# Delta gates computed in pieces inside the delta layer's input projection, and another order of ScalarE's steps in attention

## What is computed

```python
def deltanet_mixer(h, s0_fwd, s0_bwd, w_in, conv_w, a_log, dt_bias, norm_g, w_o):
    proj = h @ w_in                       # 4096 columns of q, k, v, z and 32 columns of gates
    qkv, z, gate_a, gate_b = jnp.split(proj, [...], axis=-1)
    ...
    log_decay = -jnp.exp(a_log) * jax.nn.softplus(gate_a + dt_bias)
    beta = jax.nn.sigmoid(gate_b.astype(jnp.float32).reshape(b, t, 2, DN_HEADS))
    o_f, s_f = gated_delta_chunked(q, k, v, log_decay[:, :, 0], beta[:, :, 0], s0_fwd)
    ...

def gated_delta_chunked(q, k, v, g, beta, s0):   # chunks of 64 tokens
    g = jnp.cumsum(g, axis=-1)            # within a chunk; exp(g), exp(g_last - g), exp(g_last) follow
    ...

def one_block(q_blk):                     # attention, 128 queries at a time
    s = jnp.einsum('bqhgd,bkhd->bhgqk', q_blk, k).astype(jnp.float32) * scale
    p = jax.nn.softmax(s, axis=-1).astype(v.dtype)
    return jnp.einsum('bhgqk,bkhd->bqhgd', p, v)
```

## Time and profile before

| | us |
|---|---|
| median of three runs | 5915.29 |
| lowest and highest run | 5910.57, 5921.78 |
| the profiled execution's own time | 5911.5 |
| its span, first to last instruction | 5909.7 |
| TensorE busy in the span | 5230.6 (89%) |
| VectorE, ScalarE, GpSimd busy | 2408.0, 1886.3, 593.0 |
| mean granted TensorE clock | 0.931 |

### The profile page before, as it was taken

The page is one execution under the profiler, slowest core; times in us unless marked ns, Lnnn a source line. Parts: engine busy times, 40 slices in busy tenths (PEclk is TensorE's granted clock), DMA queues, the critical chain, the costliest instruction groups (busy, mean ns, idle before and its releaser), DMA issues. The chain is left out here.

```text
span 5909.7 us, 148888 instructions
## 1 busy us (share of the span) xinstructions
PE 5230.6 (89%) x66464; PEld 4736.3 (80%) x66464; DVE 2408.0 (41%) x4332; ACT 1886.3 (32%) x3895; POOL 593.0 (10%) x1104
## 2 busy tenths in 40 slices
PE   6797999988998887999885887899887999988998
PEld 2386888877997766999884776799877888877997
DVE  0242454534334364333214553433452545544334
ACT  1032343333223354222323332322322443433223
POOL 0002232200000000000002221000001232310000
PEclk8798999988998898999896997899998999988999
DMA  9731000011221301221322111122021000011221
GB/s 406 316 116 45 23 19 22 17 54 58 79 71 50 65 2 58 79 72 50 111 77 64 39 44 69 51 74 75 32 108 63 21 17 25 15 43 56 79 71 53
DMA packets 99690, 411.65 MB, mean 70 GB/s; under 512 B 18011, under 2 KB 33755, under 8 KB 69918
## 3 DMA queue, kind: packets, MB, share of 16 engines
q1 hardware_dynamic: 87590, 376.71, 18.4%
q10 hardware_dynamic: 11520, 26.22, 1.1%
HBM read 358.20 MB, written 39.44 MB: 67 GB/s over the span
## 5 line engine op out<-in xcount | busy, mean ns | idle before, releaser
L372 PE MATMUL bank<-src_hi,ring_hi 128*128 128x320 f32 x4032 | 933.2, 313 | 177.0 <-DVE ring_lo L353 128.5
L372 PE MATMUL bank<-src_lo,ring_hi 128*128 128x320 f32 x4032 | 929.8, 312 | 4.7 <-issue 4.7
L372 PE MATMUL bank<-src_hi,ring_lo 128*128 128x320 f32 x4032 | 928.0, 312 | 0.0
L372 PEld LDWEIGHTS bank<-src_hi,ring_hi 128*128 128x128 f32 x4032 | 683.3, 191 | 184.7 <-issue 171.8
L372 PEld LDWEIGHTS bank<-src_hi,ring_lo 128*128 128x128 f32 x4032 | 683.9, 190 | 5.0 <-issue 5.0
L372 PEld LDWEIGHTS bank<-src_lo,ring_hi 128*128 128x128 f32 x4032 | 684.5, 191 | 0.0
L592 ACT ACTIVATE stage<-bank 128x320 f32<-128x320 f32 x512 | 196.2, 435 | 1398.4 <-PE bank L372 1398.4
L364 DVE TENSOR_TENSOR ring_lo<-ring,ring_hi 128x2048 fp32r<-128x2048 f32 x178 | 407.5, 2289 | 521.4 <-ACT ring_hi L360 520.5
L372 PE MATMUL bank<-hidden_hi,ring_lo 128*128 128x320 f32 x2048 | 466.7, 309 | 0.0
L372 PE MATMUL bank<-hidden_hi,ring_hi 128*128 128x320 f32 x2048 | 466.5, 309 | 0.0
L372 PE MATMUL bank<-hidden_lo,ring_hi 128*128 128x320 f32 x2048 | 466.5, 309 | 0.0
(11 more groups left out here) (396 smaller groups left out, 8607.8 us busy)
## 6 DMA issues: line engine op xcount, KB each, us to landing
ring<-w_mlp SPq DMA_DIRECT2D x124, 1024.0 KB, 4.8
mod_ring<-w_mod SPq DMA_DIRECT2D x48, 2048.0 KB, 11.8
ring<-rw_wrkv SPq DMA_DIRECT2D x22, 1024.0 KB, 5.1
rkv<-stage ACTq DMA_DIRECT2D x48, 320.0 KB, 2.6
ring<-dn_win SPq DMA_DIRECT2D x15, 1024.0 KB, 5.3
r_k<-rkv SPq DMA_DIRECT2D x32, 320.0 KB, 3.4
dn_proj<-stage ACTq DMA_DIRECT2D x32, 320.0 KB, 3.9
src<-mixed SPq DMA_DIRECT2D x24, 320.0 KB, 7.3
```

Of the source, the lines that this page charges most:

```text
L372: last = self.nc.tensor.matmul(acc[h][:, 0:HALF], wt[:, n % 2, k, m * P:(m + 1) * P], x[:, k, h * HALF:(h + 1) * HALF], start=first and q ...
```

## The change

Two edits. In attention, ScalarE's order within a step becomes: copy of (n, 0), both exponentials of n + 1, copy of (n, 1).

```diff
                     for n in range(NPT):
-                        for e in range(2):
-                            if n + 1 < NPT:
+                        transposed_out(n, 0)
+                        if n + 1 < NPT:
+                            for e in range(2):
                                 exponentials(n + 1, e)
-                            transposed_out(n, e)
+                        transposed_out(n, 1)
```

```diff
-                    projection(nc, g, d["dn_win"], 16, out=d["dn_proj"])
-                    delta_gates(nc, g)
+                    delta_input(nc, g, d["dn_win"], d["dn_proj"])
...
+def delta_input(nc, g, w, out):
+    N_SLABS, DEEP = 16, 2
+    RATES, TIMES, SUMS_AT, ENDS, NEGATED, TURNED = 4, 5, 7, 9, 10, (11, 12, 13, 14)
...
+        tmp = ed[:, :].rearrange("p (a t) -> p a t", a=2)
...
+        acc, raw_l, raw_c, turned = [(bank[0], bank[1]), (bank[2], bank[3])], bank[4], bank[5], bank[6:8]
...
+                for n in range(1, N_SLABS):                      # SP
+                    ring.load(sp, 0, 0, n)
+                    if n == 4:
+                        sp.wait_ge(s["raw_out"], 1)
+                        sp.dma_start(g.d["dn_gates"]..., raw[0:4 * DN_HEADS, :]).then_inc(s["raw_stored"], 16)
+                        sp.wait_ge(s["raw_stored"], 16)
+                        for a in range(2):
+                            sp.dma_start(ab[H8, a, :, :], ...).then_inc(s["raw_loaded"], 16)
...
+                for n in range(N_SLABS):                         # TensorE
+                    if n:
+                        pe.wait_ge(s["wl_ready"], n + 3)
+                    for m in range(2):
+                        u = 2 * n + m
+                        pe.wait_ge(s["evacuated"], u + 1)
+                        for k in range(NB):
...
+                            last = ring.product(acc[u % DEEP], n, m, k, x_hi, x_lo, k == 0, k == NB - 1)
+                        last.then_inc(s["mm_done"], 1)
+                    if n == 1:
+                        gate_sums()
+                    if n in TURNED:
+                        turn_rows(TURNED.index(n))
...
+                def evacuate(u):                                 # ScalarE
+                    act.wait_ge(s["mm_done"], u + 5)
+                    if u >= DEEP:
+                        act.wait_ge(s["stored"][u % DEEP], 16 * (u // DEEP))
+                    for h in range(2):
+                        last = nc.scalar.copy(stage[:, u % DEEP, h * HALF:(h + 1) * HALF], acc[u % DEEP][h][:, 0:HALF])
+                    last.then_inc(s["evacuated"], 1)
+                    act.wait_ge(s["evacuated"], u + 1 + DEEP)
+                    act.dma_start(out[u], stage[:, u % DEEP, :]).then_inc(s["stored"][u % DEEP], 16)
...
+                for n in range(N_SLABS):
+                    if n + 1 < N_SLABS:
+                        ring.upper(act, 0, 0, n + 1)
+                    evacuate(2 * n)
+                    if n == 2:
+                        raw_gates()
+                    if n == TIMES:
+                        rates()
+                    if n == ENDS:
+                        decays()
+                    evacuate(2 * n + 1)
+                    if n == TIMES:
+                        betas()
+                    if n in TURNED:
+                        columns_out(TURNED.index(n))
...
+                for n in range(N_SLABS):                         # VectorE
+                    if n + 1 < N_SLABS:
+                        ring.rest(dve, 0, 0, n + 1)
+                    if n == RATES:
+                        rate_inputs()
+                    if n == SUMS_AT:
+                        running_sums()
+                    if n == NEGATED:
+                        dve.wait_ge(s["decays"], 2)
+                        nc.vector.tensor_scalar(nb[H8, :], rows[H8, R_EG:R_EG + TT], -1.0, ...).then_inc(s["scaled"], 3)
```

More of the change, by code:

```diff
@@ L2273, in _ @@
             def _(sp):
[L2274 to L2280, removed]
+                ring.load_first(sp, FRONT)
@@ L2287, in _ @@
+                sp.wait_ge(s["gates_stored"], 16 * (DN_HEADS + 1))
             @block.tensor
             def _(pe):
[L2289 to L2293, removed]
@@ L2320, in _, with raw_gates @@
[L2320 to L2325 removed]
+                def raw_gates():
+                    act.wait_ge(s["raw_ps"], 1)
+                    nc.scalar.copy(raw[0:4 * DN_HEADS, S_LAT], raw_l[0:4 * DN_HEADS, :])
+                    nc.scalar.copy(raw[0:4 * DN_HEADS, S_CTX], raw_c[0:4 * DN_HEADS, 0:CTX]).then_inc(s["raw_out"], 1)
@@ new lines, in decays @@
+                def decays():
+                    act.wait_ge(s["sums"], 1)
+                    nc.scalar.activation(rows[H8, R_EG:R_EG + TT], rows[H8, R_G:R_G + TT], ACT.Exp).then_inc(s["decays"], 1)
+                    nc.scalar.activation(rows[H8, R_EL:R_END].rearrange("p (u e) -> p u e", e=2), pairs(R_G)[:, :, :, C - 1],
+                                         ACT.Exp).then_inc(s["decays"], 1)
+                    act.wait_ge(s["sums"], 2)
+                    nc.scalar.activation(ed[H8, :], ed[H8, :], ACT.Exp).then_inc(s["scaled"], 1)
@@ new lines, in _ @@
+                act.sem_inc(s["evacuated"], DEEP)
+                for b in range(NB):
+                    for ap, cols_ in token_parts(g.h, b):
+                        last = nc.scalar.copy(x_hi[:, b, cols_], ap)
+                    last.then_inc(s["hi_ready"], 1)
+                    if b in (2, 3):
+                        ring.upper_first(act, (FRONT, BACK)[b - 2])
+                for n in range(N_SLABS):
[13 more added lines that the diff above has]
+                        columns_out(TURNED.index(n))
@@ L2327, in _ @@
+                for u in range(DEEP):
+                    act.wait_ge(s["stored"][u], 16 * (2 * N_SLABS // DEEP))
             @block.vector
@@ L2356, in _, with rate_inputs @@
-                dve.wait_ge(s["decays"], 2)
-                nc.vector.tensor_scalar(nb[H8, :], rows[H8, R_EG:R_EG + TT], -1.0, None, ALU.mult).then_inc(s["scaled"], 3)
+                def rate_inputs():
+                    dve.wait_ge(s["raw_loaded"], 32)
+                    dve.wait_ge(s["g_loaded"], 32)
+                    for e in range(2):
+                        last = nc.vector.tensor_scalar(ab[H8, 0, e, :], ab[H8, 0, e, :], small[H8, 2 + e:3 + e], None, ALU.add)
+                    link(last)
+                    link(nc.vector.tensor_scalar(tmp[H8, :, :], ab[H8, 0, :, :], -1.0, None, ALU.mult))
+                    nc.vector.tensor_tensor(tmp[H8, :, :], tmp[H8, :, :], ab[H8, 0, :, :], ALU.max).then_inc(s["rate"], 1)
```

134 lines of the change are left out of this document (76 added, 58 removed).

## The result

The changed kernel takes 5863.08 us, a median of four runs (5861.52 to 5866.12), beside 5913.93 for the kernel before: a ratio of 0.9913, 95% interval 0.9896 to 0.993. Later, on another occasion, six runs gave 5865.79 beside 5907.08: 0.9926, 0.9913 to 0.994. The prediction was 5868, range 5857 to 5884. The profiled execution of the changed kernel took 5861.59 us, its span is 5859.8 (before: 5911.5 and 5909.7), and its mean granted clock 0.935 for 0.931.

What follows compares the result with a forecast made beforehand. Bounds: TensorE in the delta projection, a latency chain in the gates, TensorE waiting for ScalarE's copy in attention. 5911.5 - 52.8 + 11.7 - 6 = 5864.4 profiled, so 5868 median; range 5857 to 5884.

Steps and rivals of the forecast that it cites:

- gate sums on TensorE: In the delta projection: eight blocks of a 512 and a 128 column product, 1.08 each, add 8.6 us.
- transposes on TensorE: In the delta projection: four groups of ten at full clock, 0.65 each, add 2.6 us, bounds 2.5 and 4.9.
- five changes between kinds of product: In TensorE's stream in the projection: switching between kinds of product adds 0.5 us, bounds 0 to 1.
- pieces on ScalarE, VectorE, SP: Gate work between the projection's evacuations, casts and splits fits the free time, longest on ScalarE 5.3 of 6.29 us: nothing added.
- two accumulators, straight code: In the projection: two accumulators instead of four leave 6.3 us to spare, and unrolling the loop is no slower: nothing added.
- attention: Full steps go from 5.48 to 5.21 us; 20 steps plus 0.6 beside short tiles save 6, bounds 0 and 9.
- The phase that goes: The gates' own phase between projection and heads, barrier and semaphore clearing included, disappears from the path: 52.8 us saved.
- costed at nothing: In the projection: ScalarE, VectorE and SP gate work, fewer accumulators and unrolled code were each taken to add no time.
- second rival: In the projection: gate work waiting across engines stalls TensorE, bringing back up to 26 us, 5894 in all; chance 0.12.
- third rival: In the projection: late evacuations idle TensorE, clock halves, units up to 7 us longer, 5980 with half; chance 0.04.
- The walk: One attention step timed from its scores' start: copy 2.71, exponentials 3.28 and 4.16, next scores 5.21 us.
- The median: Whole kernel: runs' median lies 3.8 us above the profiled execution, so 5864.4 becomes 5868.

Runs made afterwards that it cites:

- straight code: Kernel before with the delta projection as straight code with two accumulators, gates still a separate phase, old attention order: median 5905.28 us beside 5909.49.
- one accumulator: Changed kernel with one accumulator instead of two in the projection, each unit waiting for the previous copy: 5890.16 us, one run; projection and gates 281.13.
- longer pieces: Changed kernel with useless extra ScalarE copies between the two evacuations of slabs 3, 6 and 8: 5880.84 us, one run; projection and gates 257.93.
- delta alone: Changed kernel with the old attention order, so only the delta gates moved: median 5875.48 us beside 5909.49 for the kernel before, ratio 0.9937.

## Why the prediction was right, step by step

| term | predicted | measured |
|---|---|---|
| gate sums on TensorE | 8.6 | 8.64 |
| transposes on TensorE | 2.6 (2.5 to 4.9) | 4 x 0.62 = 2.5 |
| five changes between kinds of product | 0.5 (0 to 1) | 0.30 + 4 x 0.29 = 1.46 |
| pieces on ScalarE, VectorE, SP | 0 | 0 |
| two accumulators, straight code | 0 | -0.2 to 0 |
| projection and gates in all | -41.1 | -40.4 |
| attention | -6 (0 to -9) | -6.0 (-6.8 in the first pair) |
| both | -47.1 | -46.4 |

**The phase that goes.** As said: the heads' first load now follows the last evacuation by 3.97 us (3075.22 to 3079.19), and nothing new stands between. 40.40 saved and 12.58 added (8.94 and four times 0.91) make 52.98 for the phase, 52.8 in the prediction; the 0.2 between them lies ahead of the first evacuation, which comes 15.84 behind the first load for 16.02 before, as it does in the straight code alone (15.81).

**TensorE's share.** The sums came out to the tenth. So did the transposes: the choice of the halved time, from line 2019, over the whole 1.23 was right, as 123 ns a piece at 0.50 became 62 at 1.00. The price by columns that the Trainium skill gives ("TensorE: Matmul & The Clock Gate", section "LDWEIGHTS (loading the stationary operand)"), a formula with no clock in it that makes 107 ns for 128 columns, does not hold here: 40 transposes cost 2.5 us, not 4.3. The step that failed is the changes between kinds of product: I saw no gap inside the gate sums and took 0.1 for a change from one stream to another. The gate sums alternate two shapes of one type; going from the projection's products to float32 work and back costs 0.29 to 0.30, three times what I put in, and 1.46 for all five is outside my bounds of 0 to 1. Doubling the transposes separated the two. What in it costs the time stays open: one accumulator shows that 0.11 of it comes behind a mere stop as well.

**What was costed at nothing** cost nothing. For the evacuations the reason was tested and holds: longer pieces show that ScalarE could be kept 12.6 us between two evacuations, 6.3 of it hidden by the time to the next evacuation and 6.3 by the second accumulator. The second rival (gates not hidden) would have needed pieces more than twice as long. How much later the cast, VectorE's half of the split or SP's load could come was not tried; for them only the absent waits speak.

**The third rival** was priced wrongly on both sides. Stops of 0.8 to 0.9 us in each unit left the clock alone, which the rival took to fall; and one stop of 4.49 us did lower it, but the unit lost 2.8 us, not 7.

**Attention.** The walk gave 2.71 for the copy, 3.28 and 4.16 for the exponentials, and 5.21 for the next scores; the trace has 2.70, 3.29, 4.16 and 5.19. From the second context tile on the count was right as well: a round of five tiles takes 24.80 for 25.76, where three full steps give 0.29 each and the two steps at the context tile 0.1 together. Five such rounds give 4.8, and the one ahead of them, 25.51 for 27.30, gives 1.8: 6.6 us. That the stage gained 6.0 on the mean, and not more, comes from the round ahead of these, where the sum had no term for the clock. At its start TensorE waits for the diagonal of the first context tile. The kernel before, and straight code with two accumulators, which has the same order in attention:

```profile
2039.35 2.50 PE L2060 MATMUL probs_t<-diag,probs 128*128 128x128 f32 x10 [2.32 <-DVE diag L2191]
```

```profile
2037.48 1.38 PE L2060 MATMUL probs_t<-diag,probs 128*128 128x128 f32 x10 [1.26 <-DVE diag L2191]
```

The granted clock in the 3 us from there on is 0.50 in the first and 1.00 in the second, and the same ten products take 2.50 and 1.38. The round took 31.78 in the kernel before, 29.96 in the straight code and 29.76 in delta alone (a wait of 1.49, clock 1.00). In all eight profiles with the new order the wait was 1.62 to 2.41, the clock fell to 0.50 as well, and the round took 31.08 to 31.87. On the mean that is 0.9 more for the new order, which takes back part of the 6.6; a gain of 0.3 ahead of this round gives the rest of the 6.0. Whether the new order makes this wait longer cannot be told from three profiles of the old one. That the 6.0 meets the 6 of the sum is luck in this part.

**The median.** I added 3.8 for the way the profiled execution of before stood to its median. The changed kernel's profiled execution stood 1.5 below its own. Over all runs this offset is scatter of the rest of the program and carries nothing. Without it the forecast would have been 5864, 1 above the first median, but with 18 us of scatter in the rest such closeness is chance; what the prediction got right is the sum of the stages. The range has a slip: the terms named for its lower end, -3 and -5, lead from 5868 to 5860 and not to 5857. The result lies above both.

## What to carry to other kernels

A small latency chain that has a phase of its own can be cut up and put behind the steps of a neighbouring phase that one engine bounds: it then costs only what it adds on that engine, plus, in this kernel, some 0.3 us for each place where its stream of products is broken by another kind, so few places with more work each are better than many. Before giving buffers away, work out how long a piece may keep the evacuating engine (time to the next evacuation, plus a unit, less the copy, for a spare accumulator; one spare was tried here) and place pieces below that. And where several stages change, compare the stages by their first loads, since the scatter of the rest can be larger than what is looked for.

## What the runs showed of the hardware that I had not expected

- Going from float32r products with 128 columns of weights to float32 work and back costs 0.29 to 0.30 us, though TensorE shows no wait there; the pieces are 0.09, 0.09 and 0.11 us in the starts of neighbouring rows. With one accumulator, 0.07 to 0.11 of this kind shows behind a stop with no change of product, too.
- The clock kept 1.00 through 26 stops of 0.84 or 0.94 us, one in 8 us, and fell to 0.50 after one of 4.49. After stops of 2.53 us in attention it fell in some steps and not in others with the same wait; at the first context tile it fell after waits of 1.62 to 2.41 us and not after 1.26 and 1.49. What decides between them was not looked into.
- After 12.93 us of standing TensorE began the gate sums at 0.50, and after 16.80 us the changed kernel's first products too (0.50 from 2835 to 2839). Here it paid to give it work in that time that has to be done anyway: the gate sums in front cost 3.4 us less than behind slab 1.
